# A mixture-of-experts stage in plain fp32, in blocks of 64 tokens, with w1 and w3 in the two column halves of the PE array

## The reference, cut to what matters

```
def expert_block(args):
    e, tok, g = args
    xb = ht[tok]                                          # rows of 1024
    hid = jax.nn.silu(xb @ w1[e]) * (xb @ w3[e])          # w1, w3: 1024 x 512
    return (hid @ w2[e]) * g[:, None].astype(ht.dtype)    # w2: 512 x 1024
```

```
layer 0: 48 48 43 37 99 63 153 177 77 70 76 41 148 145 134 177   (1536)
layer 1: 44 16 42 26 44 82 125 95 37 37 55 19 110 42 112 138     (1024)
```

## Time and profile before

| | us |
|---|---|
| median of 3 runs (1637.46 to 1643.38) | 1641.4 |
| profiled execution | 1641.5 |
| its span, first to last instruction | 1639.8 |
| PE busy (86% of the span) | 1403.7 |
| DVE busy (68%) | 1111.4 |
| ACT busy (44%) | 714.6 |
| bytes moved by DMA, MB | 357.57 |

### The profile page before, as it was taken

The page is one execution under the profiler, slowest core; times in us unless marked ns, Lnnn a source line. Parts: engine busy times, 40 slices in busy tenths (PEclk is TensorE's granted clock), DMA queues, the critical chain, the costliest instruction groups (busy, mean ns, idle before and its releaser), DMA issues. The chain is left out here.

```text
span 1639.8 us, 20695 instructions
## 1 busy us (share of the span) xinstructions
PE 1403.7 (86%) x6750; PEld 985.6 (60%) x6751; DVE 1111.4 (68%) x1475; ACT 714.6 (44%) x822; POOL 163.1 (10%) x144
## 2 busy tenths in 40 slices
PE   4788989457967899999999299799996789999990
PEld 2454555224446788888887144388653678878770
DVE  2379999974777886596553451376556788888844
ACT  3101101042345685585552330166433567777732
POOL 0000000000321010011010200000002101112201
PEclk9899999778988999999999599899997899999995
DMA  9457456308017997799564600040161799999935
GB/s 342 150 194 250 152 206 230 115 22 326 39 39 282 356 399 268 274 400 398 207 256 165 265 1 0 21 83 2 25 245 39 281 365 399 398 399 397 399 137 192
DMA packets 164095, 357.57 MB, mean 218 GB/s; under 512 B 7776, under 2 KB 35152, under 8 KB 164048
## 3 DMA queue, kind: packets, MB, share of 16 engines
q1 hardware_dynamic: 148848, 301.39, 50.3%
q0 software_dynamic: 8784, 31.99, 5.1%
q10 hardware_dynamic: 6416, 23.60, 3.6%
HBM read 318.57 MB, written 38.37 MB: 218 GB/s over the span
## 5 line engine op out<-in xcount | busy, mean ns | idle before, releaser
L717 DVE TENSOR_TENSOR W_LO<-W_RAW,W_HI 128x2048 fp32r<-128x2048 f32 x192 | 433.5, 2287 | 136.4 <-ACT W_HI L710 129.1
L710 ACT ACTIVATE W_HI<-W_RAW 128x2048 fp32r<-128x2048 f32 x192 | 363.0, 1912 | 97.8 <-DMA W_RAW<-in_moe_w 54.7
L1406 PE MATMUL PS<-W_HI,XLO 128*128 128x512 f32 x624 | 252.8, 405 | 28.3 <-DVE XLO L1541 28.2
L1408 PE MATMUL PS<-W_HI,XHI 128*128 128x512 f32 x624 | 247.7, 397 | 0.0
L1407 PE MATMUL PS<-W_LO,XHI 128*128 128x512 f32 x624 | 247.6, 397 | 0.0
L1184 PE MATMUL PS<-HT,RING 128*128 128x512 f32 (+1 forms) x512 | 174.6, 497 | 8.5 <-DVEq L1255 8.5
L1406 PEld LDWEIGHTS PS<-W_HI,XLO 128*128 128x128 f32 x624 | 120.0, 192 | 57.8 <-issue 25.9
L1184 PEld LDWEIGHTS PS<-HT,RING 128*128 128x128 f32 x512 | 97.6, 195 | 88.4 <-issue 72.7
L1408 PEld LDWEIGHTS PS<-W_HI,XHI 128*128 128x128 f32 x624 | 120.0, 192 | 26.2
L1407 PEld LDWEIGHTS PS<-W_LO,XHI 128*128 128x128 f32 x624 | 120.0, 192 | 23.7
L1406 PE MATMUL PS<-W_HI,HLO 128*128 128x512 f32 x312 | 124.8, 400 | 3.4 <-ACT YO L1497 3.4
(11 more groups left out here) (238 smaller groups left out, 1809.7 us busy)
## 6 DMA issues: line engine op xcount, KB each, us to landing
W_RAW<-in_moe_w SPq DMA_DIRECT2D x192, 1024.0 KB, 11.0
RING<-in_w_mod SPq DMA_DIRECT2D x24, 2048.0 KB, 14.3
moe_out<-YO ACTq DMA_DIRECT2D x39, 512.0 KB, 6.2
moe_out<-HT SPq DMA_DIRECT2D x20, 512.0 KB, 8.4
RING<-in_conv_pw SPq DMA_DIRECT2D x16, 512.0 KB, 5.3
ROWS<-rows_of_layer SPq DMA_DIRECT2D x12, 512.0 KB, 6.4
RING<-in_attn_w_qkv SPq DMA_DIRECT2D x3, 2048.0 KB, 8.1
moe_in<-RING SPq DMA_DIRECT2D x10, 512.0 KB, 3.0
```

The lines of the kernel that those rows point to most:

```text
L710: nc.scalar.activation(part(W_HI[q], p), part(WRAW[q], p), ACT.Copy).then_inc((w2_hi if q == 2 else w_hi)[L], 1)
L717: nc.vector.tensor_tensor(part(W_LO[q], p), part(WRAW[q], p), part(W_HI[q], p).bitcast(F32), ALU.subtract).then_inc(lo[L], 1)
L1406: pe.matmul(to, lo, W_HI[q][:, at:at + 512], start=start, stop=False)
L1408: return pe.matmul(to, hi, W_HI[q][:, at:at + 512], start=False, stop=stop)
```

## The change

Blocks have `SUB` = 64 tokens. There is no split into high and low parts: `XT`, `HTT` and the weights are plain fp32. The array's columns are used in two halves: w3's product goes to PSUM partitions 0 to 63 and w1's to 64 to 127 of one bank, by `tile_position=(0, g * SUB)`; `down` puts the two halves of w2's output columns side by side in the same way. Loads are three DMAs of 2 MB per expert. From expert 1 on they land in one of two raw places by turns, and ACT (w1, half of w2) and DVE (w3, half of w2) copy them to the one place that PE reads (`place`). Expert 0 is loaded straight to that place. Where the raw place is comes from a third row of the `INFO` table (`HOME`). The loads of the stage start at the first gather (`xg_in` at 16). The tables of the router have 64 lanes and 192 or 128 cells. In the diff below the first `block_step` is ACT's and the second DVE's.

```diff
+SUB = P // 2
+DEEP_SUB = [2 * TILES, 2 * LT]
+MAXB = [2 * TILES * P // SUB + NE, 2 * LT * P // SUB + NE]
...
+        def load_weight(sp, L, e, kind):
+            name, landed = {1: ("moe_w1", w1_in), 2: ("moe_w2", w2_in), 3: ("moe_w3", w3_in)}[kind]
+            if e:
+                sp.wait_ge(landed[L], e * 16)
+                at = {1: 4 + 2 * (e % 2), 3: 5 + 2 * (e % 2), 2: 8 * (e % 2)}[kind]
+            else:
+                at = {1: 2, 3: 3, 2: 1}[kind]
...
-                    sp.wait_ge(xg_in[L], 32)
-                    load_weights(sp, L, 1, (0, 1))
-                    load_weights(sp, L, 0, (2,))
+                    sp.wait_ge(xg_in[L], 16)
+                    load_weight(sp, L, 0, 2)
+                    for e in range(1, NE):
+                        for kind, placed in ((1, (w1_placed,)), (3, (w3_placed,)),
+                                             (2, (w2_placed_low, w2_placed_high))):
+                            if e >= 3:
+                                for one in placed:
+                                    sp.wait_ge(one[L], (e - 1) * (1 if kind == 2 else 2))
+                            load_weight(sp, L, e, kind)
...
-                        pe.matmul(to, lo, W_HI[q][:, at:at + 512], start=start, stop=False)
-                        pe.matmul(to, hi, W_LO[q][:, at:at + 512], start=False, stop=False)
-                        return pe.matmul(to, hi, W_HI[q][:, at:at + 512], start=False, stop=stop)
+                    def up(load, half_way):
+                        for k in range(KT):
+                            if k % 4 == 0:
+                                pe.wait_ge(w3_placed[L], load * 2 + (1 + k // 4))
+                                pe.wait_ge(w1_placed[L], load * 2 + (1 + k // 4))
+                            for g, w in enumerate((W3, W1)):
+                                ins = pe.matmul(PUV[g * SUB:(g + 1) * SUB, :], XT[:, k, :], w[:, k * FE:(k + 1) * FE],
+                                                start=(k == 0), stop=(k == KT - 1), tile_position=(0, g * SUB))
+                            if k == 3:
+                                half_way()
+                        ins.then_inc(up_done[L], 1)
...
+                            for c in range(2):
+                                at = k * D + c * 512
+                                ins = pe.matmul(PYO[c * SUB:(c + 1) * SUB, :], HTT[:, k, :], W2[:, at:at + 512],
+                                                start=(k == 0), stop=(k == FE // P - 1), tile_position=(0, c * SUB))
...
+                def place(eng, copy, L, load, home, kind, halves, placed):
+                    at, landed = {1: (home + 4 * WSLOT, w1_in), 3: (home + 5 * WSLOT, w3_in), 2: (home * 4, w2_in)}[kind]
+                    to = {1: W1, 2: W2, 3: W3}[kind]
+                    eng.wait_ge(landed[L], load * 16 + 16)
+                    for p in halves:
+                        copy(to[:, p * PART:(p + 1) * PART], WR[:, bass.ds(at + p * PART, PART)]).then_inc(placed[L], 1)
...
+                    def block_step(b, rows, again_):
+                        before, load = expert_of(act, b - 1), expert_of(act, b)
+                        take_hid(b - 1)
+                        silu(b, True)
+                        x_low(b + 1)
+                        up_next(load, b)
+                        y_store(b - 1, rows, again_)
+                        down_next(before, load, b)
...
+                    def block_step(b):
+                        before, load = expert_of(dve, b - 1), expert_of(dve, b)
+                        hid(b, True)
+                        x_high(b + 1)
+                        up_next(load, b)
+                        down_next(before, load, b)
```

More of the change, by code:

```diff
@@ L349, in build @@
         blocks_turned = both("blocks_turned")
[L351 to L356, removed]
+        w1_in = both("w1_in")
+        w3_in = both("w3_in")
+        w2_in = both("w2_in")
+        w1_placed = both("w1_placed")
+        w3_placed = both("w3_placed")
+        w2_placed_low = both("w2_placed_low")
+        w2_placed_high = both("w2_placed_high")
         idx_set = both("idx_set")
@@ L692, in build @@
         WRF = RING[:, 1, 3 * D + 512:4 * D].rearrange("p (s k e) -> p s k e", s=2, k=KT)
[L693 to L725, removed]
-                kn = FE // P if q == 2 else KT
-                for p in range(2):
-                    half = slice(p * kn // 2, (p + 1) * kn // 2)
-                    sp.dma_start(part(WRAW[q], p).rearrange("p (k f) -> p k f", k=kn // 2),
-                                 src[e][:, half, :]).then_inc((w1_in, w3_in, w2_in)[q][p], 16)
+        PART = WSLOT // 2
+        def load_weight(sp, L, e, kind):
[5 more added lines that the diff above has]
+                at = {1: 2, 3: 3, 2: 1}[kind]
+            k = FE // P if kind == 2 else KT
+            sp.dma_start(WR[:, at * WSLOT:(at + 1) * WSLOT].rearrange("p (k f) -> p k f", k=k),
+                         a[name][L].rearrange("e (k p) f -> e p k f", p=P)[e]).then_inc(landed[L], 16)
         def gather(pool, L):
@@ new lines, in up_next, with down_next @@
+                    def up_next(load, b):
+                        after = expert_of(act, b + 1)
+                        home = home_of(act, b + 1)
+                        with act.If(load < after):
+                            place(act, copy, L, after, home, 1, (0, 1), w1_placed)
+                    def down_next(before, load, b):
+                        home = home_of(act, b)
+                        with act.If(before < load):
+                            place(act, copy, L, load, home, 2, (0,), w2_placed_low)
@@ L1551, in hid_lo @@
[L1551 to L1572 removed]
+                    n = blocks_of(dve, L)
@@ new lines, in up_next, with down_next @@
+                    def up_next(load, b):
+                        after = expert_of(dve, b + 1)
+                        home = home_of(dve, b + 1)
+                        with dve.If(load < after):
+                            place(dve, copy, L, after, home, 3, (0, 1), w3_placed)
+                    def down_next(before, load, b):
+                        home = home_of(dve, b)
+                        with dve.If(before < load):
+                            dve.wait_ge(down_done[L], b)
+                            place(dve, copy, L, load, home, 2, (1,), w2_placed_high)
```

410 lines of the change are left out of this document (183 added, 227 removed).

## The result

The changed kernel takes 1650.08 us (median of 4 runs, 1648.77 to 1651.09). The kernel before, on the same chip, takes 1640.65 (4 runs, 1637.46 to 1643.38). The ratio is 1.0054, with a 95% interval of 1.0039 to 1.0068: 9 us slower, where 1627 us had been forecast.

What follows compares the result with a forecast made beforehand. Layer 0 was taken as bound by PE, layer 1 by PE and DMA together. Layer 0 +4.2 us, layer 1 -15.6 and the surroundings -2.8 gave -14.2, so 1627 us; own range 1618 to 1638, whole range 1600 to 1675.

Steps and rivals of the forecast that it cites:

- rival 1: Expert stages: rows land late and bound the step, 13.4 us; 1687 us total, 1657 if half the steps; chance 0.26.
- rival 2: PE products: column halves do not overlap at 512 columns, step 22.4 us, about 2140 us total; chance 0.03.
- 399 GB/s taken: Weight and row loads in the expert stages: DMA stays near 399 GB/s, 17.1 us per expert with one block.
- 4.6 us taken: End of each layer's expert stage: turn, copy and product of the last block take 4.6 us.
- 10.3 + 1.3 + 0.5 = 12.1: PE's step per 64-token block: products 10.3 us, twelve transposes 1.3, four changes of array shape 0.5; 17.68 before.
- The 0.4 us to spare: Steps with a new expert: ACT's copy of w1's first half is ready 0.4 us before PE needs it.
- its wait of 2.6 us: Layer 1: PE waits about 2.6 us for expert 12's weights, after four single-block experts.
- A microsecond more in the step is 46 us more in all: Both expert stages: PE's step counts in 28 + 18 blocks, so each extra microsecond adds 46 us.
- rival 3: PE's step: changing array shape costs nothing, step 11.6 us, total 1604 us; chance 0.17 for a step near 11.6.
- 20.7 was forecast: Start of each expert stage: expert 1 begins 20.7 us in, after 6.3 MB of weights, rows, landing and first copy.
- +4.2: Layer 0's expert stage: it ends at 909.3 us instead of 905.1, losing 4.2 us to its DMA-bound start.
- forecast 2.8: Around the expert stages: last copies and stores -0.4 us twice, first combine wait -3.0, router tables +1; sum -2.8 us.

Runs made afterwards that it cites:

- experiment 6: Experiment 5's kernel with all products of w3 ahead of all of w1, instead of alternating: 1925.23 us, ratio 1.1734 to the kernel before.
- Experiment 1: Changed kernel with each block's 64 rows gathered as 128 half rows into 128 partitions: 1630.94 us, ratio 0.9932 to the kernel before.
- experiment 7: Changed kernel with no gather in the expert stages but the first, all blocks using block 0's rows: 1641.96 us, ratio 1.0004 to the kernel before.
- experiment 2: Changed kernel with weights loaded in DMAs of 1 MB instead of 2 MB: 1651.57 us, ratio 1.0058 to the kernel before.
- experiment 5: Changed kernel with rows gathered into 128 partitions, eight narrow transposes, and the last block's hidden-row copy on DVE: 1618.66 us, ratio 0.9869 to the kernel before.
- Experiment 3: Changed kernel with each layer's last copy of hidden rows on DVE instead of ACT: 1637.04 us, ratio 0.9972 to the kernel before.

## Why the prediction was wrong

Slower had been given 0.29, all of it to late rows (rival 1) and to halves that don't overlap (rival 2), and neither came. What made the kernel slower is in no rival: two terms of the sum failed, the DMA rate (399 GB/s taken, 377 measured) and the last block of each layer (4.6 us taken, 11.2 and 10.8 measured).

**The step of PE: right in kind, and better than forecast.** The pairs overlap, with 16 records in 3.65 us, and experiment 6 shows that they do. The forecast summed 10.3 + 1.3 + 0.5 = 12.1; measured are 11.6, and 11.9 with a new expert. The term too large is that of the transposes. I left the twelve at 1.29 us because their stationary side keeps 128 columns; with 64 moving columns they take 0.64 + 0.39 from start to start. What the changes of shape cost was not measured by itself; with 3 x 3.43 = 10.3 for the products and 1.0 for the transposes, 0.3 us are left for them in a step of 11.6, where 0.5 had been estimated. The 0.2 us more in a step with a new expert are a wait for the copies. The 0.4 us to spare that the prediction counted there did not exist, in part because the shorter transposes bring PE to the next block earlier.

**The DMA rate: the term that failed, with its size.** The prediction took 399 GB/s from the earlier trace rows for a kernel whose gather goes to other partitions, and said that DMA "should stay near 399". It read 377. Everything that DMA sets in the forecast was therefore too early. Experiment 1 returned the rate by spreading the same bytes, experiment 7 by leaving them out, experiment 2 excluded the size of the loads. In layer 1, from the first transposes on:

| | forecast | after | experiment 5 |
|---|---|---|---|
| first product of expert 5 | 89.0 | 95.1 | 90.9 |
| first product of expert 11 | 197.9 | 209.9 | 203.8 |
| first product of expert 12 | 212.6 | 226.4 | 220.4 |
| first product of expert 14 | 248.9 | 263.9 | 256.1 |
| last turn of hidden rows | 309.4 | 322.5 | 313.5 |
| end of the stage | 314.0 | 333.2 | 318.9 |

The forecasts of experts 11 to 14 are its own steps of 12.1 us from expert 5 on, with its wait of 2.6 us in front of expert 12. At full rate expert 12 is 7.8 us late, not 13.8. So the rate is not all. In experiment 5 DMA had gaps here, and the adding of the prediction has none (the columns are those of rows 1):

```profile
1440.00:1450.00 10.00, 10.00 (x54) 3.39 (x50) 4.51 (x5) 6.54 (x7) 1.16 (x2) 1.00 0.77 275
```

The share is 0.77, and 0.84 from 1420 to 1430 us, where 1.04 is full: about 5 us of DMA time in all. SP issues no load between 1425.6 and 1441.1 us, and the next one goes out when ACT's copy of w2 ends, which frees its raw place. With experts of one block, two raw places per matrix were not always enough to keep DMA busy. No run has a third one, so what it would give is open.

**A shorter step in front of DMA gives next to nothing.** PE's steps from expert 5 to 11 were 0.2 to 0.5 us shorter than forecast, and PE waited for experts 11, 12 and 14 in layer 1: 6.61 + 1.82 + 2.25 = 10.7 us in the changed kernel and 6.28 + 2.35 + 1.03 = 9.7 in experiment 5, where 2.6 had been added up. "A microsecond more in the step is 46 us more in all" held for layer 0's 28 blocks and for the 5 from expert 14 on in layer 1, not for the 13 in front of them. The steps of rival 3, 11.6 us, came nearly true, and its 1604 us did not.

**The start.** Expert 1 begins 22.7 us after the first transposes in layer 0, 22.9 in layer 1, where 20.7 was forecast; 17.8 and 18.0 us an expert followed instead of 17.1. Layer 0 was DMA-bound at the start as forecast; its 28 later blocks, with steps shorter than 12.1, took 8 us less than forecast and paid for all this, so its sum, +6.6 against +4.2, is nearly right for partly wrong reasons.

**The tail: a step missing from the sum.** "Turn, copy and product of the last block, 0.4 + 0.8 + 3.4 = 4.6" took the copy's duration and forgot what is queued ahead of it on ACT. In the loop that place is harmless, since half a step of PE lies behind it. Behind the last block nothing does: 4.7 us of wait where 0.8 had been put, and 5.6 to 6.0 for the records where 3.4 had, 6.6 and 6.2 us over the forecast. Experiment 3 shows it by itself.

**What held.** POOL and the gathers were never late (rival 1 false; rows landed after 6.8 us in the median of layer 0, against 7.4 for twice the rows). The copies on DVE take 1.22 us, less than the 1.5 taken and far from the bound of 2.29:

```profile
L1534 DVE COPY WR<-WR 128x2048 f32 x90 | 106.4, 1224 | 131.8 <-DMA WR<-in_moe_w 74.2 <-PE PS L1416 44.2 <-issue 13.4
```

Their idle time before is mostly a wait for DMA: the copies were not the limit, the loads were. Between and after the stages 3.8 us went away (forecast 2.8). For them the forecast named the first combine work's wait in layer 0, 8.82 us before; it is 8.09 now, so the saving is mostly not where it was put.

```profile
927.14 1.15 ACT L1617 ACTIVATE RING<-RING,GATE 128x1024 f32<-128x1024 f32 x1 [8.09 <-DMA RING<-moe_out,DST]
```

In sum: of the 23 us between the forecast of 1627 and the time of 1650, the two costs not foreseen are the rate, 14 us by the places named in experiment 1, and the tails, 13 us by experiment 3. The shorter step gave back 8 us in layer 0, and the waits at the start of both layers took some of it again. Without both, and with the faster transposes, the kernel takes 1619, within the forecast's own range of 1618 to 1638. That isn't the forecast come true: its step is 11.4 to 11.6 us, and its experts 11 to 14 of layer 1 still come 6 to 8 us late.

## What to carry over

When a tile is halved, look at which partitions its transfers now reach, not only at its bytes: a small gather into 64 partitions lowered the rate of everything beside it by 5%. A full DMA's rate is a measured property of a mix of transfers and doesn't pass unchanged from one kernel to the next. And the order within an engine that is free in the loop should be read again for the last block, where its whole length is on the path and what follows runs slower after the pause.

## What the chip showed beyond expectation

- A gather of 64 rows into partitions 0 to 63 beside full-width loads brings the total rate from 395 down to 377 GB/s at the same DMA share, 1.04. As 128 half rows in 128 partitions: 395 to 396. Without any: 396.
- fp32 products of 512 columns in alternate halves of the array's columns: 16 records in 3.65 us; in the same half 7.08.
- Eight fp32 transposes of 64 rows by 128 columns: 0.64 us to the next start from one half of the array's rows, 0.40 from both halves in two groups of four. Four of 128 by 128: 0.58.
- After a pause of 4.7 us sixteen records took 5.6 and 6.0 us in the changed kernel (granted clock 0.57 over the 8 us of the slower one) and 5.0 and 5.2 in experiment 1; after one of 1.35 us they took 3.65 at 1.00.
